# Three pairs of FFN chunks as seven block products in a two-layer decoder kernel

## The reference, cut to what matters

```
def rms_norm(x, g):
    y = xf * lax.rsqrt(jnp.mean(xf * xf, axis=-1, keepdims=True) + EPS)
    return (y * g)

def swiglu(h, w_in, w_out):                  # w_in 1024 x 5632, w_out 2816 x 1024
    a, b = jnp.split(h @ w_in, 2, axis=-1)
    return (jax.nn.silu(a) * b) @ w_out

x = x + 0.5 * swiglu(rms_norm(x, norm_g[l, 0]), ffn_w_in[l, 0], ffn_w_out[l, 0])
x = x + mixer(rms_norm(x, norm_g[l, 1]), ...)
x = x + 0.5 * swiglu(rms_norm(x, norm_g[l, 2]), ffn_w_in[l, 1], ffn_w_out[l, 1])
```

## Time and profile before

| | |
|---|---|
| time, 3 runs | median 1053.43 us (1053.39 to 1054.06) |
| the profiled execution | 1053.35 us, of which the span is 1051.4 us |
| PE busy | 1040.1 us, 99% of the span, 5156 matmuls |
| DVE, ACT, POOL busy | 598.2 us (57%), 525.5 us (50%), 73.4 us (7%) |
| clock that TensorE was granted | 0.995 of full on average |
| transfers | 182.45 MB, mean 174 GB/s |

### The profile page before, as it was taken

How to read it: one execution, slowest core, us unless ns; L and a number is a source line. 1 busy time by engine, 2 the same in 40 slices (tenths; PEclk the granted TensorE clock), 3 DMA queues, 4 the chain that set the end, 5 groups by cost and what they waited for, 6 DMA issues and landing times.

```text
span 1051.4 us, 14153 instructions
## 1 busy us (share of the span) xinstructions
PE 1040.1 (99%) x5156; PEld 865.4 (82%) x5156; DVE 598.2 (57%) x833; ACT 525.5 (50%) x692; POOL 73.4 (7%) x108
## 2 busy tenths in 40 slices
PE   9999999999999999999999999999999999999997
PEld 7888888888888888888888888888888888888886
DVE  5554454677576564455467765544566656445544
ACT  7434434657475554434456554344356655443443
POOL 0041000000013000000000291000000000000000
PEclk9999999999899999999999999999999999999999
DMA  7686757457401366555545665555446146655541
GB/s 243 239 214 208 218 187 249 145 175 225 136 2 41 120 202 198 191 168 199 183 150 188 221 204 193 184 198 190 170 160 200 42 140 201 199 183 177 199 160 41
DMA packets 128709, 182.45 MB, mean 174 GB/s; under 512 B 5960, under 2 KB 100272, under 8 KB 128544
## 3 DMA queue, kind: packets, MB, share of 16 engines
q1 hardware_dynamic: 127040, 176.18, 50.5%
q0 software_dynamic: 1456, 5.72, 2.4%
q10 hardware_dynamic: 176, 0.05, 0.0%
HBM read 180.34 MB, written 1.59 MB: 173 GB/s over the span
## 4 chain that ended last, share of the span: by engine, by line
PE 97%; DVE 2%; ACT 1%; issue 0%; POOL 0%; POOLq 0%; DVEq 0%; ACTq 0%
PE inb L403 16%; PE inb L405 16%; PE inb L404 16%; PE acc L403 13%; PE acc L405 13%; PE acc L404 13%; PE acc L613 2%; PE tb L512 2%; PE tb L625 2%; PE inb L640 2%; PE inb L637 1%; PE tb L592 1%; PE tb L397 1%; PE acc L397 0%; DVE tlo L1346 0%; PE inb L824 0%
## 5 line engine op out<-in xcount | busy, mean ns | idle before, releaser
L1329 DVE TENSOR_TENSOR wlo<-raw,whi 128x2048 fp32r<-128x2048 f32 x108 | 250.0, 2315 | 233.6 <-ACT whi L935 233.6
L935 ACT CAST whi<-raw 128x2048 fp32r<-128x2048 f32 x108 | 206.5, 1912 | 217.5 <-PE acc L405 117.8
L403 PE MATMUL inb<-whi,thi 128*128 128x512 f32 x720 | 281.7, 391 | 0.0
L405 PE MATMUL inb<-whi,tlo 128*128 128x512 f32 x720 | 280.5, 390 | 0.0
L404 PE MATMUL inb<-wlo,thi 128*128 128x512 f32 x720 | 280.2, 389 | 0.0
L405 PEld LDWEIGHTS inb<-whi,tlo 128*128 128x128 f32 x720 | 135.1, 188 | 28.4
L404 PEld LDWEIGHTS inb<-wlo,thi 128*128 128x128 f32 x720 | 135.2, 188 | 28.0
L403 PEld LDWEIGHTS inb<-whi,thi 128*128 128x128 f32 x720 | 135.2, 188 | 28.0
L1312 DVE TENSOR_TENSOR wlo<-raw,whi 128x2048 fp32r<-128x2048 f32 x55 | 129.1, 2352 | 43.8 <-ACT whi L922 43.5
L403 PE MATMUL acc<-whi,ghi 128*128 128x512 f32 x320 | 128.5, 402 | 0.0
L405 PE MATMUL acc<-whi,glo 128*128 128x512 f32 x320 | 125.1, 391 | 0.0
(11 more groups left out here) (231 smaller groups left out, 980.1 us busy)
## 6 DMA issues: line engine op xcount, KB each, us to landing
raw<-in_ffn_w_in SPq DMA_DIRECT2D x174, 512.0 KB, 4.7
raw<-in_ffn_w_out SPq DMA_DIRECT2D x88, 512.0 KB, 4.0
raw<-in_nsa_w_in SPq DMA_DIRECT2D x20, 512.0 KB, 4.1
raw<-in_fox_w_kvf SPq DMA_DIRECT2D x16, 512.0 KB, 4.3
raw<-in_nsa_cmp_w SPq DMA_DIRECT2D x8, 512.0 KB, 4.8
raw<-in_nsa_w_out SPq DMA_DIRECT2D x8, 512.0 KB, 4.5
raw<-in_fox_w_q SPq DMA_DIRECT2D x8, 512.0 KB, 4.5
raw<-in_fox_w_out SPq DMA_DIRECT2D x8, 512.0 KB, 4.6
```

The lines of the kernel that those rows point to most:

```text
L403: pe.matmul(o, lh, rh, start=start, stop=False, skip_group_check=True)
L405: return pe.matmul(o, ll, rh, start=False, stop=stop, skip_group_check=True)
L935: act.copy(whi[u % RING][:, :], raw[u % RING][:, :]).then_inc(s_hi, 1)
L1329: dve.tensor_tensor(wlo[u % RING][:, :], raw[u % RING][:, :], whi[u % RING][:, :].bitcast(F32), ALU.subtract).then_inc(s_lo, 1)
```

## The change: seven products in place of eight

The 11 chunks of an FFN are now taken in eight segments, `KINDS = "nnsnsnsn"`: "n" is a single chunk as before, "s" a pair of chunks (2 and 3, 5 and 6, 8 and 9). For a pair, the first matrix product has 256 tokens, 1024 rows of weights and 1024 columns; cut in halves each way it is a 2 x 2 by 2 x 2 block product, 8 block products of 12 matmuls. They are replaced by seven (Winograd's form of Strassen's scheme):

- Four blocks of tokens are sums and differences of the quarters A11, A12, A21, A22 (`S1` to `S4`). They are made once in each FFN, in the second chunk: GpSimd joins `thi` and `tlo` (`join_tokens`), VectorE multiplies by the row factor (which TensorE has spread over a row, `rstd_rows`), forms the four sums, and both split them.
- Four blocks of weights are sums and differences of the quarters b11, b12, b21, b22 (`t1`, `t3`, `t2`, `t4`), made by VectorE for each pair, 128 x 2048 each. The quarters lie in buffers of their own (`nat`, `xn`, `work`), loaded by SyncE two at a time behind other loads.
- Seven products M1, M5, M2, M6, M3, M7, M4, of one unit and 12 matmuls each. Each of them goes through the ring as a unit: a cast and a subtraction of 128 x 2048. ScalarE and VectorE add them up (`m1`, `m5`, `u2`, `c12`, `u3`, `c22`, `c21`).

An FFN has 42 units instead of 33, of which 21 go through `raw`. The hidden of a pair is turned in two halves (`pair_turn`). The output products keep their 24 matmuls; those of a chunk stand one or two segments later than its input products. All loops are written out. GpSimd's decay additions wait until unit b of the last single chunk of FFN 2 is used, because their buffer `low` holds FFN 2's tokens and weight sums.

```diff
+KINDS = "nnsnsnsn"
+LOADS_AT_ONCE = 2
+def ffn_order():
+    order = []
+    for kind, j, rows in SEGMENTS:
+        if kind == "n":
+            order += [("a", j), ("b", j)] + [("o", r) for r in rows]
+        else:
+            order += [("M1", j), ("M5", j), ("o", rows[0]), ("M2", j), ("M6", j)]
+            order += [("o", r) for r in rows[1:]] + [("M3", j), ("M7", j), ("M4", j)]
+    return order + [("o", r) for r in LAST_ROWS]
...
+            def product(f, j, name, a, bank, start, stop):
+                u = U_FFN[f] + UNIT_OF[name, j]
+                a_hi, a_lo = token_block(a)
+                pe.wait_ge(s_lo, u + 1)
+                for k in range(4):
+                    col = slice(k * CW, (k + 1) * CW)
+                    mm = three(bank[:, :], a_hi[:, k], a_lo[:, k], whi[u % RING][:, col], wlo[u % RING][:, col],
+                               start and k == 0, stop and k == 3)
+                mm.then_inc(s_used, 1)
...
+            def ffn_pair(f, j, rows):                                  # TensorE
+                n = len(PAIRS) * f + PAIRS.index(j) + 1
+                product(f, j, "M1", "A11", inb[1], True, False)
...
+                product(f, j, "M5", "S1", tb[1], True, False)
+                out_rows(f, rows[0])
+                pe.wait_ge(s_m1, n)
+                product(f, j, "M2", "A12", inb[1], False, True)
...
+                product(f, j, "M6", "S2", inb[0], True, False)
+                for r in rows[1:]:
+                    out_rows(f, r)
...
+                pe.wait_ge(s_m5, n)
+                product(f, j, "M3", "S4", tb[1], False, True)
...
+                pe.wait_ge(s_u2, n)
+                product(f, j, "M7", "S3", inb[0], False, True)
+                pe.wait_ge(s_c12, n)
+                product(f, j, "M4", "A22", tb[1], True, True)
+                pair_turn(f, j, 0)
...
+            def token_sums(f):                                         # VectorE
+                m = whole_tokens(f)
+                dve.wait_ge(s_whole, 2 * f + 2)
+                dve.wait_ge(s_rc, f + 1)
+                for t in range(NT):
+                    tok = slice(t * P, (t + 1) * P)
+                    dve.tensor_tensor(m[:, :, tok], m[:, :, tok],
+                                      rstd_row[:, tok].unsqueeze(1).broadcast_to([P, KT, P]),
+                                      ALU.mult).then_inc(s_an, 1)
+                dve.wait_ge(s_an, 2 * f + 2)
+                a11, a12, a21, a22 = [quarter(m, a) for a in ("A11", "A12", "A21", "A22")]
+                dve.tensor_tensor(four(c22), a21, a22, ALU.add).then_inc(s_as, 1)
...
+                dve.tensor_tensor(a12, a12, a11, ALU.subtract).then_inc(s_as, 1)
...
+                dve.tensor_tensor(combined(f), b12, b11, ALU.subtract).then_inc(s_tw, 1)      # t1
...
+                dve.tensor_tensor(b12, b22, b12, ALU.subtract).then_inc(s_tw, 1)              # t3
...
+                dve.tensor_tensor(b11, b12, b11, ALU.add).then_inc(s_tw, 1)                   # t2
...
+                dve.tensor_tensor(combined(f), b21, b11, ALU.subtract).then_inc(s_tw, 1)      # t4
...
             pool.wait_ge(s_cq, 1)
+            join_tokens(2)
+            pool.wait_ge(s_used, U_FFN[2] + UNIT_OF["b", PAIRS[-1] + 2] + 1)
```

More of the change, by code:

```diff
@@ L67, with ring_loads @@
 U_FFN = [U_FFN0, U_FFN1, U_FFN2, U_FFN3]
+def ring_loads():
+    count, last, loads = [0] * RING, [None] * RING, {}
+    for u in range(U_END):
+        if not any(b <= u < b + FFN_UNITS and ORDER[u - b][0] not in "abo" for b in U_FFN):
+            slot = len(loads) % RING
+            count[slot] += 1
+            loads[u] = (slot, count[slot], last[slot])
+            last[slot] = u
+    return loads
+LOADS = ring_loads()
+SPLITS = ["S1", "S2", "S4", "S3"]
 TURNS = ["ffn0", "nsa", "ffn1", "kv", "ffn2", "fox", "ffn3"]
@@ L312, in _, with load @@
         def _(sp):
[L313 to L317 removed]
+            def load(u, halves):
+                slot, count, last = LOADS[u]
+                if last is not None:
+                    sp.wait_ge(s_lo, last + 1)
                 for dst, src in halves:
[L319 removed]
+                    sp.dma_start(dst, src).then_inc(s_raw[slot], 16)
             def ffn_in(f, j, half, u):
@@ L481, in last_chunk, with rstd_rows @@
                         mm.then_inc(s_tile0, 1)
-            def out_part(slot, t, k, first=False):
-                for n in range(2):
-                    mm = out_columns(slot, t, k, n, first=first)
-                return mm
-            def out_columns(slot, t, k, n, last=False, first=False):
-                h_hi, h_lo = (ghi_last, glo_last) if last else (ghi, glo)
+            def rstd_rows(name):
+                pe.wait_ge(s_rstd, NORMS.index(name) + 1)
+                for t in range(NT):
+                    mm = pe.matmul(tb[1][:, t * P:(t + 1) * P], rstd[:, t:t + 1].broadcast_to([P, P]),
+                                   ident[:, :], start=True, stop=True)
+                mm.then_inc(s_rrow, 1)
@@ L498, in out_last, with out_rows @@
+            def out_rows(f, j):
+                u = U_FFN[f] + UNIT_OF["o", j]
+                pe.wait_ge(s_lo, u + 1)
+                pe.wait_ge(s_glo, NTURNS * f + turns_before(j + 1))
+                for t in range(NT):
+                    for k in range(2):
+                        for n in range(2):
+                            mm = out_columns(u, j, t, n, k, first=j == 0 and k == 0)
+                mm.then_inc(s_used, 1)
+            def out_last(u, j, t):
                 for n in range(2):
-                    out_columns(slot, t, 0, n, True)
@@ L574, in ffn @@
-                out_last((u + 3) % RING, 1)
+                for n in range(2):
+                    mm = out_columns(u, j, 1, n, 1)
+                mm.then_inc(s_used, 1)
+                out_last(u + 1, last, 1)
             def tail(cols):
@@ L1395, in ffn @@
             def ffn(f):
-                b, n0, h0 = U_FFN[f], NJ * f, (NJ + 1) * f
-                hidden(2 * n0, acc)
+                b = U_FFN[f]
+                for t in range(NT):
+                    hidden_tile(2 * NSEG * f + t, t, acc)
                 if f:
```

570 lines of the change are left out of this document (412 added, 158 removed).

## The result

The changed kernel takes 1058.0 us (median of 7 runs, 1056.3 to 1059.8), the kernel before 1054.2 (median of 7, the three of the table above among them). One of those seven took 5970 us, which no trace explains; without it the median is 1054.1. The ratio is 1.0037, 95% interval 1.0025 to 1.005: slower by 0.4%, where 1050.8 and faster was forecast. The profiled execution took 1059.84 (span 1058.1); it is the longest of the seven, 1.8 us above their median.

A forecast was written before the change was run, and what follows sets the result against it. Matmuls on TensorE, busy 99%, were taken as the bound. 1053.35 - 32.7 (matmuls) + 2.2 (added) + 26.0 (waits) + 0.8 (FFN 0's start) + 0.3 (moved work) + 0.8 (clock) + 0.1 (restarts) gives 1050.8 us, range 1041 to 1062.

The forecast's parts named there:

- Matmuls removed: Input products of pairs: 96 matmuls become 84, three pairs in four FFNs, 144 x 0.227 = 32.7 us less on the chain.
- Removing a matmul is worth that: TensorE in the FFNs: each matmul removed saves 0.227 us if its next operands are ready.
- dearer sums: Rival, VectorE's weight sums: they take longer than a split; 1065 at 2.6 us a sum, 1090 at 3.12; chance 0.17.
- A single chunk and a pair: Three chunks of an FFN: 204 matmuls and 12 transposes, 47.7 us on TensorE; 48.1 us expected in the profile after.
- Work added: TensorE: row factor products, 2.2 us in all; VectorE: extra splits and weight sums at 2.29 us, 2.21 in a row.
- The second chunk: First pair of each FFN: TensorE waits for VectorE 3.3 us at chunk 1, 1.3 at M5, 0.8 at M6; together 5.6.
- The smaller waits of the later pairs: Two later pairs of each FFN: TensorE waits 0.2 us at M6 and 0.2 at unit a, 0.9 for both pairs.
- Moved work: GpSimd's decay additions at FFN 2's end cost 0.3 us, or 4 if stretched to 44 us; token joins run in VectorE's idle stretch.
- The clock: TensorE's 3.3 us pause can halve the clock; later waits swallow most of the loss: 0.2 us per FFN, 0.8 in all.
- The rival of the clock: First pair: half rate for 6.8 us in every FFN, 2.1 of 3.4 us lost swallowed; 1055 us, chance 0.10.
- Transfers: Unit o's loads arrive at 423, ScalarE wants them at 424: free. Rival: late at 250 GB/s, 1062.8 us, chance 0.07.
- Sum: Whole kernel: all terms give -2.5 us against the profiled 1053.35, so 1050.8; chance 0.50 within 1046 to 1056.

The follow-up runs named there:

- e12_twoearly: Changed kernel with hidden buffers at the lower place and two pairs instead of three, the first where it was (nnsnsnnnn): 1061.8 us, ratio 1.0071.
- e1_lower: Changed kernel with fhi and flo allocated ahead of vx, so fhi starts at byte 168064 instead of 204992; no instruction changed: 1053.2 us, ratio 0.9994.
- e5_both: Changed kernel with fhi and flo ahead of vx and unread matmuls in TensorE's wait at chunk 1: 1050.7 us, ratio 0.9972.
- e4_busy: Changed kernel, buffers as they were, with unread matmuls in TensorE's wait at chunk 1 (12 per FFN, 20 in FFN 0): 1055.4 us, ratio 1.0014.
- e8_all128: Changed kernel with hidden buffers at the lower place and 128 unused bytes ahead of everything, all at multiples of 256: 1053.5 us, one execution.
- e7_split: Changed kernel with fhi at 168192 (multiple of 256) and flo at 209536 (128 bytes behind one): 1057.5 us, one execution.
- e11_order: Changed kernel, hidden buffers at the lower place, VectorE's M1 weight split and chunk 1's gating moved ahead of token work: 1071.2 us, ratio 1.016.

## Why the prediction was wrong

- **Matmuls removed.** That they come off the chain was right (e12_twoearly: a pair is worth 2.1 us, estimated 2.3). The step that failed is "Removing a matmul is worth that", taken as 0.227 for every matmul that stays. I priced what the change removes and adds, but not the move of the hidden columns from `ghi`, `glo` to `fhi`, `flo`, which touched all output matmuls. The missing term measured 4.8 us (e1_lower, e5_both), more than the gain of 2.5 that I forecast, so it alone turns faster into slower. A slower kernel had 0.29, but for other reasons (dearer sums, the clock, transfers); no rival named this one.
- **A single chunk and a pair.** Forecast 48.1 us. Measured 48.62 in the changed kernel, and with the buffers at the lower place 48.25. Timelines of TensorE, first matmul of unit a behind the first and the second pair of FFN 1; the changed kernel:

```profile
429.73 0.48 PE L571 MATMUL inb<-whi,thi 128*128 128x512 f32 x1
...
478.35 0.48 PE L571 MATMUL inb<-whi,thi 128*128 128x512 f32 x1
```

And e1_lower:

```profile
428.64 0.48 PE L571 MATMUL inb<-whi,thi 128*128 128x512 f32 x1
...
476.89 0.48 PE L571 MATMUL inb<-whi,thi 128*128 128x512 f32 x1
```

- **Work added.** Weight sums at 2.28 to 2.29 us on average (forecast 2.29). The rival of dearer sums falls.
- **The second chunk.** Right in place, releaser and size in FFN 1, but for M6's (0.4 where 0.8 was forecast). The smaller waits of the later pairs were 0.2 or less. FFN 0 waited 4.7 idle, forecast 3.3 + 0.8.
- **Moved work.** The decay additions (772.16 to 802.29) run past the boundary beside splits of up to 3.74 us and cost nothing that the waits of the profile after show; in e1_lower and e5_both, with the faster pace, TensorE waits 0.4 for a split of 3.2 us there, about what I counted. What I did not count: the wait of 0.56 us that they made at the start of FFN 2 is gone. The joins were priced as free, and they are, since the split that they stretch is not waited for. Timelines of GpSimd and VectorE in FFN 1:

```profile
370.32 2.39 POOL L2208 TENSOR_TENSOR kT<-thi,tlo 128x1024 f32<-128x1024 f32 x1 [1.00 <-DVE tlo L1614]
...
370.91 3.96 DVE L1586 TENSOR_TENSOR wlo<-raw,whi 128x2048 fp32r<-128x2048 f32 x1 [0.67 <-ACT whi L1154]
```

  They overlap from 370.91 to 372.71, 1.80 us, and the split is 1.67 longer than 2.29; at half speed during the overlap it would be 0.9 longer. The exclusive lock of the Trainium skill (SBUF — State Buffer, "Who interferes with whom") agrees with these two rows.
- **The clock.** "I count 0.2 per FFN, 0.8 in all": mis-sized. e4_busy measured 2.6, 1.8 more. The low stretch was 6.83 us, twice the length that I took; 1.0 to 1.8 of it fell into the pause itself, the rest cost 2.5 to 2.9, and the waits behind it swallow 1.6, not all: 0.9 to 1.3 us for each fall, where I had 0.2. The rival of the clock had the right mechanism (1055 with all four FFNs; three fell in the profiled run). The rule that I set beside it, of the Trainium skill (TensorE: Matmul & The Clock Gate, "HAM oscillation — how this bites in real kernels"), would have brought the fall back in each FFN: the trace shows it in three of four (those of e1_lower and e8_all128 in two), so the measurement decides.
- **Transfers.** Unit o's loads land after 7.7 us and no wait on them reaches TensorE. That rival falls.
- **Sum.** 1050.8 + 4.8 (place) + 1.8 (clock beyond the 0.8) = 1057.4, measured 1058.0. The 0.6 left are less than the interval of the measurement (1.3 us either way), so nothing rests on them. FFN 0's longer wait (4.7 idle and a restart against 4.1) would be as much, with small ones the other way (M6, and FFN 2's start); no run takes them apart.

## What to carry to other kernels

When a change moves a matmul's stationary operand to another buffer, compare the start-to-start distance of the matmuls that use either buffer in the trace before, and start all stationary buffers at the moving buffer's place modulo 256: every kernel here that did so had the faster pace. An engine that is free by 10% on average can still set a wait where one-off work meets its densest stretch; a chunk of distance was worth more than a third pair. And a pause of some 3 us on TensorE costs its length and then, in most cases here, a stretch at half clock: price both, and look at what is queued behind that can take it up.

## What the runs showed of the hardware

- Matmuls of 512 columns in float32r with a 128 x 128 stationary operand start 0.227 us apart when the stationary operands start at the same place modulo 256 bytes as the moving one (0 and 0, 128 and 128; upper and lower end of the partition), and 0.232 to 0.234 when they are off by 64 or 128 (mean over all in the trace, the ones behind transposes left out). In e7_split, with one of the two stationary buffers off, the matmuls with the other were slow too. It is 3% of a matmul, and hardly to be seen in durations. The Trainium skill (SBUF — State Buffer, "Who interferes with whom") gives TensorE two independent read ports, one for each operand; the pace depends on the places of both all the same, and the measurement decides.
- The clock fell to 0.50 for 6.83 us, in some runs for 3.41, behind pauses of 3.1 us idle, but not behind each one; behind those of 4.7 to 4.9 us (FFN 0) it fell in every trace, and behind the longest of e11_order (up to 6.1 us) in all four FFNs. Where unread matmuls left 0.5 us of idle it did not fall.
- Unread matmuls in a pause made the kernel faster: 2.6 us (1058.0 to 1055.4, and again 1053.2 to 1050.7 with the buffers at the lower place).
